# A hybrid decoder layer on one core: the first group's B convolved beside the samples' values, norm squares summed on GpSimd, the decay spread as one matmul

## The reference, cut to what matters

```python
hn = _rmsnorm(x, norm_w)
u = hn @ w_in
z_ssd, xbc, dt_raw, q, k, v, z_att, g_ssd, g_att = jnp.split(u, _split_points(), axis=-1)
xbc, new_conv = _causal_conv(xbc, conv_state, conv_w, conv_b)          # 4 taps, then SiLU
xs, Bm, Cm = jnp.split(xbc, [D_SSD, D_SSD + SSD_GROUPS * SSD_STATE], axis=-1)
dt = jax.nn.softplus(dt_raw + dt_bias)
y, new_ssm = _ssd_chunked(xh, dt, A, Bm, Cm, ssm_state)                # chunks of 128, 32 heads, 4 groups
y = y + d_skip[:, None] * xh
yg = (y * jax.nn.silu(z_ssd)).reshape(b, t, SSD_GROUPS, D_SSD // SSD_GROUPS)
yg = yg * lax.rsqrt(jnp.mean(yg * yg, axis=-1, keepdims=True) + EPS)   # the norm of each group
br_ssd = (yg.reshape(b, t, D_SSD) * ssd_norm_w) @ w_ssd_br
# three dilated windows of attention over keys and values (the samples: over their caches)
alpha = jax.nn.softmax(jnp.stack(lses, axis=-1), axis=-1)              # merges the three windows
o = jnp.einsum('bthdg,bthg->bthd', jnp.stack(outs, axis=-1), alpha) * jax.nn.silu(z_att)
mix = jax.nn.sigmoid(g_ssd) * br_ssd + jax.nn.sigmoid(g_att) * (o @ w_att_br)
out = x + mix @ w_out
```

## Time and profile before

| | us |
|---|---|
| median of 3 runs | 1119.04 (1116.3 to 1121.11) |
| profiled execution, time | 1121.37 |
| profiled execution, span | 1119.6 |
| PE busy (matmuls) | 1023.8 |
| DVE busy | 707.2 |
| ACT busy | 534.6 |
| GpSimd busy | 242.5 |
| granted TensorE clock, mean | 0.97 |

### The profile page before, as it was taken

The page is one execution under the profiler, slowest core; times in us unless marked ns, Lnnn a source line. Parts: engine busy times, 40 slices in busy tenths (PEclk is TensorE's granted clock), DMA queues, the critical chain, the costliest instruction groups (busy, mean ns, idle before and its releaser), DMA issues.

```text
span 1119.6 us, 21756 instructions
## 1 busy us (share of the span) xinstructions
PE 1023.8 (91%) x8474; PEld 951.4 (85%) x8474; DVE 707.2 (63%) x1113; ACT 534.6 (48%) x1273; POOL 242.5 (22%) x327
## 2 busy tenths in 40 slices
PE   3999988898989897999999999999999998599998
PEld 2999888888888885469998998998999998599998
DVE  6867575564656357745877887887855568823432
ACT  5335565555546545215456546556545667311210
POOL 0312121232323100001212112112201989100000
PEclk9999999999999998988999999999999999699999
DMA  9543353254521046652543560571497996332231
GB/s 368 226 179 114 134 203 144 77 226 152 202 101 58 29 153 216 216 208 86 231 158 130 231 256 37 226 284 45 189 353 288 352 376 265 123 111 107 76 105 49
DMA packets 30310, 198.28 MB, mean 177 GB/s; under 512 B 4536, under 2 KB 6808, under 8 KB 20704
## 3 DMA queue, kind: packets, MB, share of 16 engines
q1 hardware_dynamic: 25712, 183.35, 43.2%
q0 software_dynamic: 4496, 13.54, 3.2%
HBM read 180.16 MB, written 104.70 MB: 254 GB/s over the span
## 4 chain that ended last, share of the span: by engine, by line
PE 59%; DVE 19%; ACT 13%; issue 7%; DMA 1%; SPq 0%; DVEq 0%; ACTq 0%
PE bank L677 34%; PE bank L711 8%; PE bank L724 4%; ACT wH L1262 4%; DVE cacc L1677 3%; ACT Sx L1426 1%; DVE yL L2102 1%; DVE wL L1656 1%; PE bank L900 1%; PE bank L998 1%; PE bank L980 1%; PE bank L972 1%; PE bank L800 1%; DVE Sx L1809 1%; DVE mst L1812 1%
## 5 line engine op out<-in xcount | busy, mean ns | idle before, releaser
L1656 DVE TENSOR_TENSOR wL<-w_raw,wH 128x2048 fp32r<-128x2048 f32 (+1 forms) x63 | 148.4, 2356 | 109.1 <-ACT wH L1262 108.0
L677 PE MATMUL bank<-xH,wH 128*128 128x260 f32 x976 | 205.4, 292 | 5.8 <-DVEq L1601 3.3
L677 PE MATMUL bank<-xH,wL 128*128 128x260 f32 x976 | 197.6, 284 | 0.0
L677 PE MATMUL bank<-xL,wH 128*128 128x260 f32 x976 | 197.5, 284 | 0.0
L677 PEld LDWEIGHTS bank<-xH,wH 128*128 128x128 f32 x976 | 151.7, 190 | 16.7 <-issue 14.6
L1262 ACT CAST wH<-w_raw 128x2048 fp32r<-128x2048 f32 (+1 forms) x63 | 119.0, 1889 | 93.5 <-PE bank L677 83.8
L711 PE MATMUL bank<-wH,xH 128*128 128x256 f32 x480 | 144.4, 301 | 18.6 <-DVEq L1601 11.3
L677 PEld LDWEIGHTS bank<-xL,wH 128*128 128x128 f32 x976 | 151.8, 190 | 0.0
L677 PEld LDWEIGHTS bank<-xH,wL 128*128 128x128 f32 x976 | 151.6, 190 | 0.0
L711 PE MATMUL bank<-wL,xH 128*128 128x256 f32 x480 | 138.7, 289 | 0.0
L711 PE MATMUL bank<-wH,xL 128*128 128x256 f32 x480 | 138.4, 288 | 0.0
(11 more groups left out here) (294 smaller groups left out, 2075.2 us busy)
## 6 DMA issues: line engine op xcount, KB each, us to landing
w_raw<-in_weights SPq DMA_DIRECT2D x62, 1024.0 KB, 5.3
out_kvs<-in_cache SPq DMA_DIRECT2D x16, 2044.0 KB, 11.0
ring<-in_cache SPq DMA_DIRECT2D x48, 256.0 KB, 4.0
slot<-in_state_ssm SPq DMA_DIRECT2D x16, 512.0 KB, 5.1
out_ssm_s<-slot POOLq DMA_DIRECT2D x16, 512.0 KB, 5.5
out_kvs<-in_cache SPq DMA_DIRECT2D x8, 508.0 KB, 7.1
out_kvp<-st POOLq DMA_DIRECT2D x18, 128.0 KB, 3.9
out_kvp<-vv POOLq DMA_DIRECT2D x18, 128.0 KB, 5.3
```

Source lines behind the costliest of these rows:

```text
L677: mm = pe.matmul(bk[hf].tile[:, 0:HALF], wslot(w, i)[:, k, s * P:(s + 1) * P], x[:, k, hf * HALF:(hf + 1) * HALF], start=(k == 0 and n == ...
L1656: TT(wL[:, i % 2, 0:k * n], raw[:, i % 2, 0:k * n], wH[:, i % 2, 0:k * n].bitcast(F32), ALU.subtract)\
```

## The change

It does this:

- Squares: `gsquare` goes; a step `ysquare u` squares one unit on ACT after its gate, and for the units 1 to 3 of a group GpSimd adds the square to the first. `gnorm` is one float32 matmul (two passes) and waits for the third add.
- Decay spread: `sel3`, its load and 16 matmuls go. DVE makes from the identity an even/odd selector for 128 columns (`oddE`) and a copy of `dsS` masked for each unit (`dsM`), with two reductions, a copy and a product in `decays`; one matmul of 256 columns spreads all. PE waits for DVE's count of 3 there, ahead of it and of the chunk ends.
- Keys: the merge's banks are (0, 2, 6) and (1, 3, 7); `mergeexps` at p=1; `dt` 0 at p=5, `dt` 1 and 2 at p=6.
- Values: no spread ahead of them, all 12 between them; B's eight tiles ahead of `sampleprobs`; B's convolution (`use`) at value 2, with its constants and the conv state's load in a new step `convstate` ahead of the values; C's tiles at values 1, 5, 9, 13, 17, 21 and two behind. `valuesum` is parted: DVE's part is `valuepart`, PE's two sums stand together at the end.
- Behind the barrier: `decays`, `dtrows`, then C's convolution (`c_use`), then x's projection.
- Buffers of SBUF move so that what is alive at once doesn't overlap.

```diff
@@ -83,8 +83,8 @@
-SPREAD_FIRST = 3
-DT_AT = 6
+SPREAD_FIRST = 0
+DT_AT = 5
 HALF_DONE = (NG - 1) * B + B // 2 - 1
@@ -191,16 +191,19 @@
             out += [za_use, ("split", ITEM_AT["bc", 0])]
-        if p == 3:
+        if p == 1:
             out.append(("mergeexps",))
...
             out.append(("score", p - 1))
-        if DT_AT <= p < DT_AT + 3:
-            out.append(("dt", p - DT_AT))
+        if p == DT_AT:
+            out.append(("dt", 0))
+        if p == DT_AT + 1:
+            out += [("dt", 1), ("dt", 2)]
     out.append(("samplemax",))
...
         out.append(("spread", i))
-    out += bc_tiles[:KD - 2] + [("sampleprobs", 0), ("sampleprobs", 1), ("selfprobs",), ("dt", 3), ("split", ITEM_AT["x", 0])]
+    out += bc_tiles + [("sampleprobs", 0), ("sampleprobs", 1), ("selfprobs",), ("dt", 3), ("split", ITEM_AT["x", 0]), ("convstate",)]
+    c_tiles, c_use = tiles(("bc", 0), 1)
     late = NG * HP - SPREAD_FIRST
@@ -208,9 +211,13 @@
             out.append(("spread", SPREAD_FIRST + i * late // n))
+        if i == 2:
+            out.append(use)
+        if i % 4 == 1:
+            out.append(c_tiles.pop(0))
         if i == HALF_DONE + 1:
-            out.append(("valuesum", 0))
-    out += bc_tiles[KD - 2:] + [("valuesum", 1), ("gated",), ("barrier",), ("decays",)]
+            out.append(("valuepart", 0))
+    out += c_tiles + [("valuepart", 1), ("valuesum", 0), ("valuesum", 1), ("gated",), ("barrier",), ("decays",), ("dtrows",), c_use]
@@ -218,29 +225,31 @@
             use = proj("bc", g, unit=0)
-            out += [("ssdS", u - 1), ("ssdE", u)]
-        out.append(use)
-        use = proj("bc", g, unit=1)
-        out += [("ssdY", u - 1), ("ssdZ", u - 1)] if g > 0 else [("dtrows",)]
-        out.append(use)
+            out += [("ysquare", u - 2), ("ssdS", u - 1), ("ssdE", u), use]
+            use = proj("bc", g, unit=1)
+            out += [("ssdY", u - 1), ("ssdZ", u - 1), use]
         use = proj("x", 2 * g, unit=0)
         out += [("bc", g), use]
+        if g > 0:
+            out.append(("ysquare", u - 1))
         use = proj("x", 2 * g, unit=1)
         if g > 0:
-            out += [("gsquare", g - 1), ("ssdA", u), ("gnorm", g - 1)]
+            out += [("ssdA", u), ("gnorm", g - 1)]
         else:
...
             use = proj(kind, j, unit=0)
+            if u % PER_GROUP:
+                out.append(("ysquare", u - 1))
             out += [("ssdS", u), ("ssdE", u + 1), use]
...
     use = proj("gs", 0, unit=0)
-    out += [("ssdS", UNITS - 1), use]
+    out += [("ysquare", UNITS - 2), ("ssdS", UNITS - 1), use]
     use = proj("gs", 0, unit=1)
-    out += [("ssdY", UNITS - 1), ("ssdZ", UNITS - 1), use, ("gsquare", GROUPS - 1)]
+    out += [("ssdY", UNITS - 1), ("ssdZ", UNITS - 1), use, ("ysquare", UNITS - 1)]
     use = proj("gs", 1, unit=0)
@@ -635,9 +652,9 @@
-            return banks[(0, 1, 4)[i % 3]]
-
-        merge_banks = [banks[i] for i in (2, 6, 0, 3, 7, 1)]
+            return banks[(4, 2, 3)[i % 3]]
+
+        merge_banks = [banks[i] for i in (0, 2, 6, 1, 3, 7)]
         block = ctx.enter_context(nc.Block())
@@ -919,13 +936,10 @@
                     mm.then_inc(banks[4].filled, 1)
-                    pe.wait_ge(S["selectors3_loaded"], 16)
+                    pe.wait_ge(S["ac_parts_ready"], 3)
                     banks[5].take(pe, ("dsb",))
-                    for u in range(UNITS):
-                        mm = pe.matmul(banks[5].tile[:, u * 2 * B:(u + 1) * 2 * B], sel3[:, u, :], dsS[:, :],
-                                       start=True, stop=True)
-                    mm.then_inc(banks[5].filled, 1)
-                    pe.wait_ge(S["ac_parts_ready"], 2)
+                    pe.matmul(banks[5].tile[:, 0:UNITS * 2 * B], oddE[:, :, :].rearrange("p e d -> p (e d)"),
+                              dsM[:, :, :].rearrange("p u b -> p (u b)"), start=True, stop=True).then_inc(banks[5].filled, 1)
                     banks[6].take(pe, ("dends",))
@@ -993,10 +1007,8 @@
                     banks[7].take(pe, ("gn", g))
-                    pe.wait_ge(S["y_squared"], g + 1)
-                    for k in range(PER_GROUP):
-                        mm = pe.matmul(banks[7].tile[:, :], mean_g[:, :], sq2[k][:, :], start=(k == 0), stop=(k == PER_GROUP - 1))
-                    mm.then_inc(banks[7].filled, 1)
+                    pe.wait_ge(S["y_squares_summed"], 3 * (g + 1))
+                    pe.matmul(banks[7].tile[:, :], mean_g[:, :], sq2[0][:, :], start=True, stop=True).then_inc(banks[7].filled, 1)
                 elif op == "sprep":
@@ -1082,11 +1094,9 @@
                       .then_inc(S[f"cache_loaded{m % RING}"], 16)
-                elif op == "valuesum" and a[0] == 0:
+                elif op == "convstate":
                     sp.wait_ge(S["sample_exps"], 2)
                     sp.dma_start(stc[:, :, :, :], state_conv).then_inc(S["conv_state_loaded"], 16)
-                elif op == "decays":
-                    sp.dma_start(sel3[:, :, :], sel_in).then_inc(S["selectors3_loaded"], 16)
                 elif op == "sprep":
@@ -1232,6 +1242,13 @@
                     nc.gpsimd.tensor_copy(ZS[:, u, :], zs[:, u % 2, 0:B]).then_inc(S["z_samples_kept"], 1)
+                elif op == "ysquare" and a[0] % PER_GROUP:
+
+                    g, k = divmod(a[0], PER_GROUP)
+                    pool.wait_ge(S["y_squared"], a[0] + 1)
+                    if k > 1:
+                        pool.wait_ge(S["y_squares_summed"], 3 * g + k - 1)
+                    nc.gpsimd.tensor_tensor(sq2[0][:, :], sq2[0][:, :], sq2[k][:, :], ALU.add).then_inc(S["y_squares_summed"], 1)
                 elif op == "sread":
@@ -1528,14 +1545,12 @@
                         free(banks[5 + e])
-                elif op == "gsquare":
-                    g = a[0]
-                    act.wait_ge(S["y_gated"], PER_GROUP * (g + 1))
-                    if g > 0:
+                elif op == "ysquare":
+                    g, k = divmod(a[0], PER_GROUP)
+                    act.wait_ge(S["y_gated"], a[0] + 1)
+                    if g > 0 and k == 0:
                         banks[7].full(act, ("gn", g - 1))
-                    for k in range(PER_GROUP):
-                        ins = A(sq2[k][:, :], ygn[:, g * PER_GROUP + k, B:R], ACT.Square)
-                    ins.then_inc(S["y_squared"], 1)
+                    A(sq2[k][:, :], ygn[:, a[0], B:R], ACT.Square).then_inc(S["y_squared"], 1)
                 elif op == "gnorm":
@@ -1609,12 +1624,13 @@
                     dve.wait_ge(S["phase_ended"], PHASE_ENDS[nbar - 1])
-                    if nbar == 2:
-                        V.memset(buf[:, 0, 0:TAPS - 1], 0.0)
-                        V.memset(buf[:, 1, 0:TAPS - 1], 0.0)
-                        ch.link(TS(wcv[:, :, 0:TAPS], par[:, PW_CONV:PW_CONVB].rearrange("p (u w) -> p u w", w=TAPS), 0.5, None, ALU.mult))
-                        ch.link(TS(wcv[:, :, TAPS:TAPS + 1], par[:, PW_CONVB:PW_SNORM].unsqueeze(2), 0.5, None, ALU.mult))
-                        dve.sem_inc(S["conv_weights_ready"], 1)
+                elif op == "convstate":
+                    dve.wait_ge(S["sample_probs_turned"], 3)
+                    V.memset(buf[:, 0, 0:TAPS - 1], 0.0)
+                    V.memset(buf[:, 1, 0:TAPS - 1], 0.0)
+                    ch.link(TS(wcv[:, :, 0:TAPS], par[:, PW_CONV:PW_CONVB].rearrange("p (u w) -> p u w", w=TAPS), 0.5, None, ALU.mult))
+                    ch.link(TS(wcv[:, :, TAPS:TAPS + 1], par[:, PW_CONVB:PW_SNORM].unsqueeze(2), 0.5, None, ALU.mult))
+                    dve.sem_inc(S["conv_weights_ready"], 1)
                 elif op == "squares":
@@ -1970,6 +1986,12 @@
                     dve.sem_inc(S["ac_parts_ready"], 1)
+                    heads = con[0:HEADS, C_ID:C_ID + HEADS]
+                    V.tensor_reduce(odd[:, :], heads.rearrange("p (u e) -> p e u", e=2), AX.X, ALU.add)
+                    ch.link(V.tensor_reduce(own_pair[:, :], heads.rearrange("p (u e) -> p u e", e=2), AX.X, ALU.add))
+                    V.tensor_copy(oddE[:, :, :], odd[:, :].unsqueeze(2).to_broadcast([HEADS, 2, HD]))
+                    TT(dsM[:, :, :], dsS[:, :].unsqueeze(1).to_broadcast([HEADS, UNITS, 2 * B]),
+                       own_pair[:, :].unsqueeze(2).to_broadcast([HEADS, UNITS, 2 * B]), ALU.mult).then_inc(S["ac_parts_ready"], 1)
                     TT(dends[:, :, :], con[0:HEADS, C_ID:C_ID + HEADS].unsqueeze(2).to_broadcast([HEADS, HEADS, NT]),
```

More of the change, by code:

```diff
@@ L432, in hybrid_kernel @@
         lT = a2.tile("lT", [SLOTS, NG, T])
[L433 removed]
+        mL_ = nc.alloc_sbuf_tensor_at("mL_", [SLOTS, NG, T], F32R, offset=a2.at - 8 * NG * T)
         merge_end_ = a2.at
@@ L443, in hybrid_kernel @@
         dsS = a2.tile("dsS", [HEADS, 2 * B])
-        VD = nc.alloc_sbuf_tensor_at("VD", [P, 2, T], F32, offset=a2.at)
-        mtmp = nc.alloc_sbuf_tensor_at("mtmp", [P, T], F32, offset=a2.at + 8 * T)
-        KT = a2.tile("KT", [P, 4, HP, NKEYS + 1])
-        selfK = a2.tile("selfK", [P, NG * HP * B])
```

(36 more changed lines are left out.)

5 lines of the change are left out of this document (2 added, 3 removed).

## The result

| | before | after |
|---|---|---|
| median, us | 1120.07 (1116.3 to 1121.29) | 1101.46 (1099.21 to 1105.04) |
| profiled execution, time / span | 1121.37 / 1119.6 | 1105.04 / 1103.3 |
| PE busy | 1023.8 | 1013.1 |
| GpSimd busy | 242.5 | 269.3 |

The ratio is 0.984 (0.981 to 0.987): 18 us faster, 2.9 us above the predicted point of 1098.6 and inside the range. A second measurement, on another chip, gave 1102.77 against 1120.53, ratio 0.985 (0.982 to 0.987).

What follows compares the result with a forecast made beforehand. TensorE (PE) was taken to hold 59% of the chain, with waits on other engines. Span 1119.6 - 11.2 + 5.8 - 8.2 - 6.8 = 1099.2; the median moved equally to 1098.6 us, range 1091 to 1108.

Steps and rivals of the forecast that it cites:

- Part 1: Keys of the samples: reordered merge banks and earlier exponentials and dt cut PE's waits, 11.2 us less.
- Part 2: Values of the samples: more groups and C's passes moved in, less waits and lowered clock, 5.8 us more.
- The group's price: Value stretch: values side by side cost 0.96 us per group, 20 groups instead of 12, 7.7 us more.
- C's 48 passes: Value stretch: C's projection passes move in and cost 5.8 us.
- Part 3: Behind the second barrier: cheaper decay spread and C's projection moved away, 8.2 us less.
- the slow block: x's projection behind the second barrier takes 8.31 us as before, not 5.74, with 2.7 us of idle ahead.
- Part 4: Norms: 1.4 us less for each of three, 2.6 for the fourth, 6.8 us less in all.
- rival 3: Norms: GpSimd's adds lock DVE out, 11 us on the path, 1109.6 us; chance 0.07.
- Rival 1: Keys and norms: PE's gains only partly on the path, keys 6 us, norms 0.5, giving 1106.5 us; chance 0.13.
- Rival 2: Barrier, keys and norms: the clock stays up and norms are worth 2, giving 1093.9 us; chance 0.13.
- Rival 4: Value stretch runs at 1.2 GHz, costing 33 us if all low, giving 1132 us; chance 0.03.
- Rival 5: Behind the second barrier: the decay spread's change gives nothing, DVE's steps cost as much, 1103.6 us; chance 0.04.

Runs made afterwards that it cites:

- x2: Changed kernel with the merge's exponentials and dt's steps back at their old places, the new order of the banks kept: 1111.26 us.
- x6: Changed kernel with the dt transposes and two spreads behind x's projection of the first group instead of ahead of it: 1102.1 us, ratio to before 0.987.
- x8: x6 with the split of the next item also put behind the dt transposes' step: 1096.73 us, ratio to before 0.981.
- x0: The changed kernel measured once more, unedited, as base for other runs: 1102.77 us, ratio to before 0.9847.
- x3: Changed kernel with the decay spread as before, sixteen matmuls by loaded selectors: 1109.07 us, ratio to before 0.9921.
- x7: Changed kernel with values in fours, DVE's state steps ahead of the split in three units, x's projection ahead of the dt transposes: 1093.3 us, ratio to before 0.978.
- x9: x7 with the split also behind the dt transposes: 1088.77 us, ratio to before 0.973.
- x1: Changed kernel with the norms as before, squares together on ACT, four matmuls, no adds on GpSimd: 1106.25 us.
- x10: Changed kernel with C's tiles at values 2, 6, 10 and on, beside the spreads: 1096.10 us, ratio to before 0.980.
- x4_grouped: Changed kernel with two spreads and a tile of C together behind every fourth value: 1093.26 us, ratio to before 0.976.

## Why the prediction was right, and where it was off

**Part 1, keys: -11.2 predicted, -11.1 measured.** Its steps stood: the merge from 406.9 to 419.9, dt's operand on ACT at 421.87 (421.7), PE's wait 1.49 (1.4), the last score's end 440.3 (440.0). x2 parts it in two, and both agree to 0.1. One term was right for another reason: of the 0.7 put down to a lowered clock behind the wait only 0.3 came (one group of eight passes of 1.38 instead of 1.09; the granted clock of the stretch is 1.00), and the wait of 0.72 ahead of the last score, which the sum left out, filled its place. The cause was read from the other engines' idle, not from PE's: 10.13 and 3.42 us in the earlier trace rows.

**Part 2, values: +5.8 predicted, +7.0 measured.** The group's price (0.96) and their number (20) were right, and no bank, ring or conv state was late. The mis-sized term is C's 48 passes: I put 5.8, as in a block; six lone tiles cost 0.2 more each, 1.2 in all.

**Part 3, barrier: -8.2 predicted, -8.9 measured**, of which 0.2 are the earlier squares of part 4. x's projection began 5.07 us behind the last value step (5.0), its block took 7.84 at the lowered clock, and ended 12.9 behind `gated` (13.2). DVE's four steps took 0.85 (0.95). The forecast took the slow block since 2.7 us of idle stood ahead, and the runs bear it out: with 0.43 us of idle ahead the block took 6.0 us (x6, x8), with an idle of 1.8 to 2.3 us ahead, or just before the last passes ahead, 7.5 to 7.9 (after, x0, x3, x7, x9). Part 3 is thus a gain that left half of itself behind: 4 us more lay in the order.

**Part 4, norms: -6.8 predicted, -3.5 to -4 measured.** This is the step that failed. The mechanism was right, the new wait at `ssdY` included (1.29, 1.31, 1.29; predicted 1 to 1.5), but its terms were too good in four places, and rival 3 took its share in one of them. The pass takes 1.10 behind its wait, not 0.92. Behind the wait at `ssdY` PE has a second one, 0.33, since DVE's gate and so its emptying of the bank come late too; I stopped the chain at the first wait. In the second of the three, C's convolution held PE 0.99 us where x1 has 0.34, so that one gave 0.3: one of GpSimd's adds had made DVE's split 1.0 us longer (rival 3, below). The third had no wait ahead of the norm behind it to shorten, and gave 0.6. And "the third barrier, which PE alone sets" was false: PE waited 1.31 us for DVE there before, and 1.75 now, which eats 0.4 of the fourth norm's 2.6. The first norm's sum of 1.4 became 0.9, the three together 1.8 instead of 4.2.

What sets DVE's pace there can be read in x0_after. Chain around its first norm:

```profile
588.70 1.15 ACT Lb L1544 x4
...
589.94 1.28 ACT L1290
591.24 0.70 ACT con L1561
...
592.05 0.64 ACT con L1563
```

The norm's sum is ready at 588.98, but ACT first finishes the decay matrix and loads a table (L1290). The scale comes 4.8 us behind the norm's start, against 5.15 with four times the passes: of the 2.6 us that PE saves, the chain through the scale, `ygn`, x's convolution and the state steps keeps 0.35.

**The rivals.** Rival 1 (only partly on the path) held for the norms alone, not for the keys. Rival 2: the block behind the barrier stayed slow and the norms gave less, so no; only among the keys did the clock stay up. Rival 4: the value stretch ran at 1.00 throughout. Rival 5: x3. Rival 3, adds lock DVE out, has its mechanism in the trace and once on the path, but a price far under its 11 us. DVE's split and GpSimd's second add of a group in x0_after, in the second group and in the third:

```profile
644.10 2.29 DVE L1672 TENSOR_TENSOR wL<-w_raw,wH 128x2048 fp32r<-128x2048 f32 x1 [0.24 <-DVE zs L1726]
644.18 3.36 POOL L1251 TENSOR_TENSOR sq<-sq,sq 128x512 f32<-128x512 f32 x1 [6.19 <-ACT sq L1553]
...
724.22 1.27 POOL L1251 TENSOR_TENSOR sq<-sq,sq 128x512 f32<-128x512 f32 x1 [6.00 <-ACT sq L1553]
724.33 3.31 DVE L1672 TENSOR_TENSOR wL<-w_raw,wH 128x2048 fp32r<-128x2048 f32 x1 [0.24 <-DVE zs L1726]
```

Where the split began first it took its 2.29 us and the add waited; where the add began first, by 0.11 us, the split took 3.31; the chain of waits runs through it, the state steps and B's and C's convolutions, and PE's wait of 0.99 is for the latter. Over the kernels with adds there are 13 splits of 3.28 to 3.41 us, each with an add begun 0.01 to 0.13 us ahead of it. Twelve of them stand ahead of a convolution of C, and PE then waits 0.96 to 1.07 for it; x2 and x10 have it in two groups, and x9, where no add came first, has 0.34 in the second group and in the third. x1, without adds, has no such split. So each costs 0.65 us, and which engine comes first is a matter of a tenth of a microsecond.

The adds reach a second kind of product too. Durations (min/median/max) of DVE's product for the decay matrix, x1_old_norms and then x0_after:

```profile
L2027 DVE TENSOR_TENSOR Lb<-Lb,CBm x32: 681/691/694, 512.4 to 804.4; 128x512 f32<-128x512 f32 x32
```

```profile
L2034 DVE TENSOR_TENSOR Lb<-Lb,CBm x32: 677/691/1632, 512.0 to 802.2; 128x512 f32<-128x512 f32 x32
```

Without adds no product took over 0.694 us, with them up to 1.63; in sum 2.5 us over the 30 products behind 520 us (19.7 and 22.2). In after one such product (588.56 to 590.79, two in 2.23 instead of 1.4) lies beside GpSimd's product of `Eb` (587.12 to 589.64), which the add had pushed back; it ends 1.2 us before DVE's next input, so PE doesn't see it there. All this agrees with the rule of the Trainium skill ("SBUF — State Buffer", "SBUF: two separate sides") that whoever starts first keeps the other out: DVE loses too. The adds themselves took 2.3 us in the mean (median 2.87, at most 3.43), where I had 1.29. The last add of each group, the one that PE's norm waits for, took only 1.28 to 1.30.

## What to carry to other kernels

When a wait is taken away, follow the chain past the first new wait and to each later place where the same engine is read (the next bank, the next barrier): here 1.3 at `ssdY` was followed by 0.33 at a bank and 0.4 at the end, and half of the 10.3 us of PE's work that the norms saved went there. Small matmuls that run side by side are priced by the group: put what stands between them (spreads, tiles) together, until the engine that feeds them binds. Where work is given to GpSimd beside DVE, look at which of the two begins first: a tenth of a microsecond decided here whether DVE's split took 2.29 us or 3.3. And where work is moved ahead of a barrier or a wait, look at which of another engine's steps now stands in front of the one that frees your bank: one `split` moved behind one step turned nothing into 4 us.

## What the runs showed of the hardware that was not expected

- A block of 48 matmuls took 6.0 us at a granted clock of 1.00 behind an idle of PE of 0.43 us (x6, x8), and 7.5 to 7.9 at 0.72 to 0.77 where an idle of 1.8 to 2.3 us stood ahead of it or ahead of the few passes before it (after, x0, x3, x7, x9). Behind 1.3 and 0.33 us in sequence both came out, with the same instructions.
- Six products of a tile (x high, low) that stand between other matmuls take 0.92 us, in a row with others of their kind 0.72 to 0.75.
- Float32 matmuls with 8 columns of weights in strips of their own take as long together as one alone: one value 0.95 us to the next instruction, two 0.96 (L917 x2 and L917 x4 above), four 0.98 (x4_grouped, 453.88 to 454.86). 24 values took 47.1 us in 20 groups and 42.4 in 15.
- GpSimd and DVE held each other up by whole instructions, and the one that began first lost nothing: a GpSimd sum of 128x512 elements took 1.27 us where it began ahead of DVE's split and 2.86 to 3.43 where it began behind it, the split 3.28 to 3.41 instead of 2.29. A DVE product of 128x512 took 1.63 instead of 0.69 beside GpSimd.
